# Delta rule in 64x64 tiles, and a mixer's front in another order

## The reference

```python
qkv = jax.nn.silu(_causal_dwconv(proj[..., OFF_Q:OFF_Z], conv_w))
g = -jnp.exp(dn_a_log) * jax.nn.softplus(a + dn_dt_bias); beta = jax.nn.sigmoid(b)
# per chunk of CHUNK = 64 tokens and per head (4 heads of 128)
g_cum = jnp.cumsum(g, axis=-1)
decay = jnp.exp(jnp.where(causal, g_cum[..., :, None] - g_cum[..., None, :], -jnp.inf))
lower = jnp.where(strict, jnp.einsum("bnhcd,bnhsd->bnhcs", kb, k) * decay, 0.0)
tmat = jnp.eye(CHUNK) + lower
sol = lax.linalg.triangular_solve(tmat, rhs, left_side=True, lower=True)   # u and w
attn = jnp.where(causal, jnp.einsum("bnhcd,bnhsd->bnhcs", q, k) * decay, 0.0)
# then a scan over the four chunks with u, w, attn, qg, k_dec and the state s
# S5: x_t = A x_{t-1} + B u_t (complex, diagonal), y = Re(C x_t) + D u_t
```

## Time and profile before

| what | value |
|---|---|
| median of three runs | 1792.93 us (1792.62 to 1793.97) |
| the profiled execution: time | 1791.53 us |
| the profiled execution: span | 1789.8 us |
| mean granted TensorE clock | 0.997 |
| TensorE busy | 1763.8 us, 99% of the span |
| VectorE, ScalarE, GpSimd busy | 1042.8, 827.8, 77.8 us |

### The profile page before, as it was taken

One profiled execution on the slowest core, in us unless ns is written; L12 is line 12 of the kernel. 1 busy time (PEld: TensorE's weight loads), 2 busy tenths in 40 slices (PEclk: granted clock), 3 DMA queues, 4 the chain that ended last, 5 costly groups with the idle time before them and its releaser, 6 DMA issues.

```text
span 1789.8 us, 26939 instructions
## 1 busy us (share of the span) xinstructions
PE 1763.8 (99%) x11356; PEld 1568.9 (88%) x11356; DVE 1042.8 (58%) x1218; ACT 827.8 (46%) x914; POOL 77.8 (4%) x145
## 2 busy tenths in 40 slices
PE   8999999999999999999999999999998999999998
PEld 8998797888999899987978879998888976889996
DVE  5445466977644455554669776455676535645553
ACT  5544355553654355543555636545123124545542
POOL 0000000000000000000000001000471100000000
PEclk9999999999999999999999999999999999999999
DMA  7547255444654645472545448855244314346371
GB/s 259 188 148 267 82 181 164 156 141 149 228 188 188 211 142 188 129 281 87 180 156 163 143 142 212 198 193 209 95 166 80 114 52 132 128 155 207 108 283 58
DMA packets 194331, 293.13 MB, mean 164 GB/s; under 512 B 9298, under 2 KB 128884, under 8 KB 194244
## 3 DMA queue, kind: packets, MB, share of 16 engines
q1 hardware_dynamic: 191988, 287.72, 47.7%
q0 software_dynamic: 1936, 4.14, 2.1%
q10 hardware_dynamic: 320, 0.01, 0.0%
HBM read 289.49 MB, written 2.36 MB: 163 GB/s over the span
## 4 chain that ended last, share of the span: by engine, by line
PE 92%; DVE 4%; DMA 2%; issue 1%; ACT 1%; ACTq 0%; DVEq 0%; SPq 0%
PE acc L233 24%; PE acc L234 23%; PE acc L235 23%; PE acc L280 3%; PE acc L216 2%; DMA ring<-in_ffn_w_in 1%; PE acc L3086 1%; PE acc L488 1%; PE acc L2777 1%; PE acc L201 1%; PE acc L262 1%; PE turn L368 1%; PE acc L1338 1%; PE turn L1443 1%; PE turn L2850 1%
## 5 line engine op out<-in xcount | busy, mean ns | idle before, releaser
L455 DVE TENSOR_TENSOR w_lo<-ring,w_hi 128x2048 fp32r<-128x2048 f32 x160 | 361.7, 2290 | 207.7 <-ACT w_hi L451 207.7
L233 PE MATMUL acc<-xT_hi,w_hi 128*128 128x256 f32 x1680 | 476.9, 284 | 1.5 <-DVE xT_lo L386 0.8
L235 PE MATMUL acc<-xT_hi,w_lo 128*128 128x256 f32 x1680 | 476.3, 283 | 0.0
L234 PE MATMUL acc<-xT_lo,w_hi 128*128 128x256 f32 x1680 | 476.2, 283 | 0.0
L451 ACT ACTIVATE w_hi<-ring 128x2048 fp32r<-128x2048 f32 x160 | 301.0, 1911 | 142.4 <-PE acc L235 99.6
L233 PEld LDWEIGHTS acc<-xT_hi,w_hi 128*128 128x128 f32 x1680 | 323.0, 192 | 2.6 <-DVE xT_lo L386 1.8
L234 PEld LDWEIGHTS acc<-xT_lo,w_hi 128*128 128x128 f32 x1680 | 323.1, 192 | 0.0
L235 PEld LDWEIGHTS acc<-xT_hi,w_lo 128*128 128x128 f32 x1680 | 323.0, 192 | 0.0
L233 PE MATMUL acc<-w_hi,hT_hi 128*128 128x512 f32 x440 | 172.7, 393 | 0.0
L235 PE MATMUL acc<-w_hi,hT_lo 128*128 128x512 f32 x440 | 171.6, 390 | 0.0
L234 PE MATMUL acc<-w_lo,hT_hi 128*128 128x512 f32 x440 | 171.5, 390 | 0.0
(11 more groups left out here) (553 smaller groups left out, 2944.2 us busy)
## 6 DMA issues: line engine op xcount, KB each, us to landing
ring<-in_ffn_w_in SPq DMA_DIRECT2D x88, 1024.0 KB, 5.7
ring<-in_w_in SPq DMA_DIRECT2D x52, 1024.0 KB, 5.0
ring<-in_ffn_w_out SPq DMA_DIRECT2D x44, 1024.0 KB, 6.4
ring<-in_w_branch SPq DMA_DIRECT2D x12, 1024.0 KB, 5.0
ring<-in_w_out SPq DMA_DIRECT2D x12, 1024.0 KB, 5.0
ring<-in_w_gate SPq DMA_DIRECT2D x11, 1024.0 KB, 5.1
ring<-in_w_up SPq DMA_DIRECT2D x11, 1024.0 KB, 6.5
ring<-in_w_down SPq DMA_DIRECT2D x11, 1024.0 KB, 6.8
```

What stands on the lines that cost most here:

```text
L233: pe.matmul(o, a_hi, wh, start=start, stop=False)
L234: pe.matmul(o, a_hi, wl, start=False, stop=False)
L235: return pe.matmul(o, a_lo, wh, start=False, stop=stop)
L455: vec.tensor_tensor(w_part(w_lo, r), raw_part(c0, r), w_part(w_hi, r).bitcast(F32), ALU.subtract).then_inc(f.lo, 1)
```

## The change

It does four things.

The delta rule's block matrices lose their zero blocks: they become 128 partitions by 64 columns, chunk b of a row tile in partitions 64b to 64b+63. Masks shrink likewise (`half_ident`, `half_upper`, copied on GpSimd at the program's start, `lvl`). Every product of two such matrices becomes two products of 64x64x64, one in each diagonal quarter of the array (`halves_pe`), both writing one PSUM bank. `dn_kk_pe` uses all 128 rows and two halves of 64 columns. The inverse's transposes become products with `half_ident`. VectorE's and ScalarE's operations there go from 512 to 256 columns.

In `rc_solve_pe` the second half now takes 64 rows at a time, chunk b to bank `turn[2 + b]`, and both banks are complete only with its last products.

The taps come ahead on all three engines: on VectorE ahead of the convolutions of keys and queries, on TensorE ahead of the values' products, on ScalarE ahead of the convolutions' activations. The memory's transposes move behind the first quarter of the values' products; the convolution of queries moves behind the memory's evictions.

The decay and the first four copies come between the two halves of the scan on VectorE; on TensorE the decay's sums come ahead of the fills, and one fill fewer stands ahead of `s5_y_pe`.

```diff
+        half_ident = sb("half_ident", [P, CH])
+        half_upper = sb("half_upper", [P, CH])
...
+        HALVES = 9
...
-        attnT = big(23588, 8, P)
+        attnT = big(23588, 8, CH)
...
-        X = big(20480, 8, P)
+        X = big(20480, 8, CH)
...
         def s5_taps_pe(pe):
             pe.wait_ge(sk.vec, TAPS)
+            pe.wait_ge(sw.act, 8)
...
+
+        def s5_scanned_vec(vec):
             vec.wait_ge(s5.vec, 5)
...
-                    ins = pe.matmul(turn[m][:, h * P:(h + 1) * P], g2[:, j:j + 1].broadcast_to([P, P]), ublk[:, :],
-                                    start=True, stop=True)
+                    for b in range(2):
+                        rows = half_rows(b)
+                        ins = pe.matmul(turn[m][rows, h * CH:(h + 1) * CH], g2[rows, j:j + 1].broadcast_to([CH, CH]),
+                                        half_upper[rows, :], start=True, stop=True)
...
-        def dn_turn_vec(vec):
-            for r in range(6):
+        def dn_copies_vec(vec, r0, r1):
+            for r in range(r0, r1):
...
+            for bank0, other in ((0, kbT), (2, qnT)):
+                for m in range(MT):
+                    for h in range(DH):
+                        for b in range(2):
+                            toks = slice(m * P + CH * b, m * P + CH * b + CH)
+                            ins = pe.matmul(turn[bank0 + m][half_rows(b), h * CH:(h + 1) * CH], knT[:, h, toks], other[:, h, toks],
+                                            start=True, stop=True)
+                    ins.then_inc(dn.pe, 1)
...
+        def halves_pe(pe, o, m, left, right):
+
+            for h in range(DH):
+                for b in range(2):
+                    rows = half_rows(b)
+                    ins = pe.matmul(o[rows, h * CH:(h + 1) * CH], left[rows, 4 * m + h, :], right(rows, 4 * m + h), start=True, stop=True)
+            return ins
...
+            for j in range(8):
+                for b in range(2):
+                    rows = half_rows(b)
+                    ins = pe.matmul(turn[2 + b][:, j * CH:(j + 1) * CH], kbe[rows, j // 4, (j % 4) * P:(j % 4 + 1) * P], XT[rows, j, :],
                                     start=True, stop=True)
-                ins.then_inc(rc.pe, 1)
+                    if j == 7:
+                        ins.then_inc(rc.pe, 1)
...
-            pe.wait_ge(rc.act, 1 + m)
+            pe.wait_ge(rc.act, 1 + n % 2)
...
-            pe.wait_ge(sw.act, 8)
-            norm_pe(pe, nmem, nb=memx)
-            turned_group_pe(pe, G_V2, C_V2, xT, 4, 512)
+            s5_taps_pe(pe)
+
+            def memory_turned(pe, half):
+                if half == 0:
+                    pe.wait_ge(sk.act, 1)
+                    norm_pe(pe, nmem, nb=memx)
+            turned_group_pe(pe, G_V2, C_V2, xT, 4, 512, between=memory_turned)
             z2_right_pe(pe)
             s5_state_pe(pe)
-            s5_taps_pe(pe)
             z2_left_pe(pe, 0)
             z2_left_pe(pe, 1)
+            dn_cs_pe(pe)
             fill(2)
-            dn_cs_pe(pe)
-            fill(1)
             dn_turn_pe(pe)
             fill(1)
...
+            s5_u_act(act)
+            s5_taps_act(act)
             conv2_act2(act, 0)
+            conv2_act1(act, 2)
             conv2_act2(act, 1)
-            s5_u_act(act)
-            conv2_act1(act, 2)
             z2_right_act(act)
-            s5_taps_act(act)
...
-            def conv_kq(vec):
+            def taps_and_conv_k(vec):
+                s5_taps_vec(vec)
                 conv2_vec(vec, 0)
-                conv2_vec(vec, 1)
...
-            s5_taps_vec(vec)
+            conv2_vec(vec, 1)
             conv2_vec(vec, 2)
             ab_vec(vec)
             s5_scan_vec(vec)
             dn_cs_vec(vec)
+            dn_copies_vec(vec, 0, 4)
+            s5_scanned_vec(vec)
+            dn_copies_vec(vec, 4, 6)
             dn_turn_vec(vec)
```

More of the change, by code:

```diff
@@ L806, in const_pool @@
                                pattern=[[-1, P]], channel_multiplier=1).then_inc(cst.pool, 1)
+            pool.wait_ge(cst.pool, 5)
+            for b in range(2):
+                rows = half_rows(b)
+                pool.tensor_copy(half_ident[rows, :], ident[rows, rows]).then_inc(cst.pool, 1)
+                pool.tensor_copy(half_upper[rows, :], upper[rows, rows]).then_inc(cst.pool, 1)
+            pool.wait_ge(cst.pool, 9)
+        HALVES = 9
         def const_vec(vec):
@@ L1868, in build @@
         HD = 128
-        CH = 64
         NS = 16
@@ L2826, in inv_start_act @@
                 act.wait_ge(iv.pe, 1 + m)
[L2827 removed]
+                act.activation(quad(X, m), heads(turn[m][:, 0:TOK], 4), ACT.Copy).then_inc(iv.act, 1)
         def inv_level_act(act, i):
@@ L2831, in inv_level_act @@
                 act.wait_ge(iv.pe, inv_p(i) + 1 + m)
-                act.activation(quad(Y, m), heads(turn[m][:, :], 4), ACT.Copy).then_inc(iv.act, 1)
+                act.activation(quad(Y, m), heads(turn[m][:, 0:TOK], 4), ACT.Copy).then_inc(iv.act, 1)
+        def halves_pe(pe, o, m, left, right):
+            for h in range(DH):
+                for b in range(2):
+                    rows = half_rows(b)
+                    ins = pe.matmul(o[rows, h * CH:(h + 1) * CH], left[rows, 4 * m + h, :], right(rows, 4 * m + h), start=True, stop=True)
+            return ins
         def inv_start_pe(pe):
@@ L2836, in inv_start_pe @@
                 pe.wait_ge(iv.vec, 2 + 2 * m)
-                for h in range(DH):
-                    ins = pe.transpose(turn[m][:, h * P:(h + 1) * P], XT[:, 4 * m + h, :], ident[:, :])
-                ins.then_inc(iv.pe, 1)
+                halves_pe(pe, turn[m], m, XT, lambda rows, j: half_ident[rows, :]).then_inc(iv.pe, 1)
         def inv_level_pe(pe, i, between):
@@ L2847, in inv_level_pe @@
                     pe.wait_ge(iv.vec, inv_v(i - 1) + 3 + 2 * m)
-                for h in range(DH):
-                    j = 4 * m + h
-                    ins = pe.matmul(turn[m][:, h * P:(h + 1) * P], CT[i % 2][:, j, :], X[:, j, :], start=True, stop=True)
-                ins.then_inc(iv.pe, 1)
+                halves_pe(pe, turn[m], m, CT[i % 2], lambda rows, j: X[rows, j, :]).then_inc(iv.pe, 1)
             between(0)
@@ L2859, in inv_level_pe @@
                 if i < 5:
-                    for h in range(DH):
-                        j = 4 * m + h
-                        ins = pe.matmul(turn[m][:, h * P:(h + 1) * P], XT[:, j, :], Y[:, j, :], start=True, stop=True)
-                    ins.then_inc(iv.pe, 1)
-                for h in range(DH):
-                    j = 4 * m + h
-                    ins = pe.matmul(turn[2 + m][:, h * P:(h + 1) * P], Y[:, j, :], XT[:, j, :], start=True, stop=True)
-                ins.then_inc(iv.pe, 1)
+                    halves_pe(pe, turn[m], m, XT, lambda rows, j: Y[rows, j, :]).then_inc(iv.pe, 1)
+                halves_pe(pe, turn[2 + m], m, Y, lambda rows, j: XT[rows, j, :]).then_inc(iv.pe, 1)
             between(1)
@@ L2874, in rc_solve_pe @@
                 for h in range(DH):
-                    ins = pe.matmul(turn[m][:, h * P:(h + 1) * P], XT[:, 4 * m + h, :], v_tok2[:, m, h * P:(h + 1) * P],
-                                    start=True, stop=True)
-                ins.then_inc(rc.pe, 1)
-            for m in range(MT):
-                for h in range(DH):
-                    ins = pe.matmul(turn[2 + m][:, h * P:(h + 1) * P], kbe[:, m, h * P:(h + 1) * P], XT[:, 4 * m + h, :],
-                                    start=True, stop=True)
-                ins.then_inc(rc.pe, 1)
+                    for b in range(2):
+                        rows = half_rows(b)
+                        ins = pe.matmul(turn[m][rows, h * P:(h + 1) * P], XT[rows, 4 * m + h, :], v_tok2[rows, m, h * P:(h + 1) * P],
+                                        start=True, stop=True)
+                ins.then_inc(rc.pe, 1)
+            for j in range(8):
+                for b in range(2):
+                    rows = half_rows(b)
+                    ins = pe.matmul(turn[2 + b][:, j * CH:(j + 1) * CH], kbe[rows, j // 4, (j % 4) * P:(j % 4 + 1) * P], XT[rows, j, :],
+                                    start=True, stop=True)
+                    if j == 7:
+                        ins.then_inc(rc.pe, 1)
         def rc_rows(n):
@@ L2914, in rc_o_pe @@
                     pe.matmul(o, qgT[:, h, n * CH:(n + 1) * CH], S2[n][:, h * P:(h + 1) * P], start=True, stop=False)
-                ins = pe.matmul(o, attnT[rows, 4 * m + h, rows], u_sol[rows, 4 * m + h, :], start=(n == 0), stop=True)
+                ins = pe.matmul(o, attnT[rows, 4 * m + h, :], u_sol[rows, 4 * m + h, :], start=(n == 0), stop=True)
             if n % 2 == 1:
@@ L2984, in rc_act @@
         def rc_act(act):
-            for m in range(MT):
-                act.wait_ge(rc.pe, 3 + m)
-                act.activation(quad(wT, m), heads(turn[2 + m][:, :], 4), ACT.Copy).then_inc(rc.act, 1)
+            for b in range(2):
+                act.wait_ge(rc.pe, 3 + b)
```

(1 more changed line is left out.)

58 lines of the change are left out of this document (28 added, 30 removed).

## The result

The median of seven runs is 1800.11 us (1795.36 to 1802.85) against 1792.89 before: a ratio of 1.0037, 95% interval 1.0027 to 1.0048. The change costs 7.2 us. I had forecast 1791.8, a gain of 1.1, with a range of 1784 to 1798.

The account below looks back on a forecast made before the run. The prediction took TensorE, busy 99% of the span, as the bound: -9.5 us behind the scan and +8.4 in the reordered front make -1.1, so the median goes from 1792.93 to 1791.8 us, range 1784 to 1798.

Parts of the forecast that it names:

- The tiles: Everything behind the scan: 64x64 products in pairs, changed solution and moved fill together save 9.5 us.
- the moved fill: One 1.75 us fill moves from before the scan to behind `rc_out_pe` and covers L233's wait: -0.95 us.
- The levels: The inverse's five levels on TensorE: 7.0 us a level instead of 8.8, -8.2 us in all.
- the solution and the first state: `rc_solve_pe` unchanged in time, but the first state product waits for a 512-column ScalarE copy: +0.7 us.
- the last wait: TensorE's 0.95 us wait at L233, the first output product, forecast to be covered by a fill.
- the diagonal pairs do not overlap: Rival, 11%: a pair of 64x64x64 products costs 0.22 us, the inverse saves nothing; 1808 us.
- TensorE at the states: TensorE reaches `s5_state_pe` at 1342.5, after taps (2.0) and 22.8 us of other work.
- The rotations' end: GpSimd's rotations, slowed by the taps' products on VectorE, end at 1335.5 to 1338.5 instead of 1322.2.
- u's landing: u is back from DRAM at 1347.7 to 1352.5, taken as 1349: TensorE waits 6.5 us at the states.
- `s5_y_pe` at S + 28.8, with a wait of some 6: S is u's landing; VectorE's copies between the scan's halves make TensorE wait some 6 us before `s5_y_pe`.
- The clock loss, 2.0 behind each wait: Lower granted clock costs TensorE 2.0 us after the wait at the states and again after `s5_y_pe`'s.
- u lands far later: Rival, 14%: last rotations fall under convolutions, u's DMAs share engines with weight loads; S = 1354, +5, 1797 us.

Follow-up runs that it names:

- the tiles alone: The changed kernel with all orders of the kernel before put back, keeping the 64x64 tiles: 1784.27 us, ratio 0.9951.
- the kernel before with its wait filled: The kernel before with 12 products that nobody reads in its 5.17 us wait ahead of the q, k, v transposes: 1792.21 us, ratio 0.9997.
- the order alone: The kernel before, on 128x128 blocks, with the change's new order and split of the scan put in: 1808.3 us, ratio 1.0078.
- after with the rows broken up: After with each half's fill in `s5_y_pe` moved into the middle of its 16 narrow products, waits unfilled: 1798.13 us, ratio 1.0029.
- its ten with the waits filled: After with 22 and 13 products that nobody reads in its waits for u and for the scan: 1794.66 us, ratio 1.0011.
- the split alone: After with taps, memory transposes and convolutions back where they were; decay and four copies stay between the scan's halves: 1792.13 us, ratio 0.9992.
- with u moved early: After with GpSimd storing u behind the sixth and loading it behind the seventh of eight rounds of rotations: 1788.47 us, ratio 0.9972.

## Where the prediction was right and where it failed

**The tiles** (-9.5, of which 0.95 by the moved fill): right. In the tiles alone, from `dn_turn2_pe` to the first output product it is 96.80 us, against 105.52: -8.7, forecast -8.55. The levels take 33.7 for 42.3, so -8.6 (forecast -8.2); from `dn_turn2_pe` to the first level 1.1 less (1.1); the solution and the first state 1.0 more (0.7); and in after the last wait is gone. A pair of products costs 0.126 with its share of the shape changes, not 0.22, so the rival "the diagonal pairs do not overlap" is out. The Trainium skill's rule in "TensorEngine Tiling (Array Packing)", "Restrictions and Gotchas", that different row tiles cannot access one PSUM bank at once, would by the prediction's rival have brought 1808; no run here shows such a price, with both halves in one bank.

**TensorE at the states** by 1342.5: right, 1343.8 less the 1.1 of the start. **The rotations' end** between 1335.5 and 1338.5: right, 1336.45 (1335.4 without the late start). The row with 2.5 us a step agrees with the Trainium skill's exclusive lock ("SBUF — State Buffer", "SBUF: two separate sides").

**u's landing** at 1349, at most 1352.5: the first step that failed. From the rotations' end to the landing I took 12.2 us from before, and at most 2 more for the weight loads. It took 16.9, because the store landed after 7.7 us instead of 3.5. It had moved to a stretch in which the DMA engines were 0.95 busy and two weight loads of 1 MB were issued; in before its stretch (1322.5 to 1326.0) was 0.74 busy. The states began at 1353.5, or 1352.4 without the late start: 3.4 late, at the far end of the bounds that I had stated.

**`s5_y_pe` at S + 28.8, with a wait of some 6:** right. 1353.5 + 28.8 = 1382.3, it was 1381.92, and the wait is 6.18. The chain of copies between the halves of the scan was read rightly.

**The clock loss, 2.0 behind each wait:** the step that failed most. I took the loss that follows before's wait as a fixed price, and had none anywhere else. In the profiled execution it was 1.5 at the states, 9.4 in `s5_y_pe` and 1.7 at the solution. From `s5_y_pe`'s start to `dn_turn2_pe` I had counted 21.4 us; it took 28.64.

Added to the forecast span of 1788.7: 1.1 for the start, 3.4 for u, -0.4 for the way to `s5_y_pe`, 7.2 in it, 0.9 behind it and 0.3 from the first output on make 1801.2; it was 1801.1. In the median the miss is 8.3 us. No median execution was traced; if u was as late there, 3.4 are from u, and the mean granted clock (0.991, against 0.989 in the profiled one) puts most of the rest on the clock too. The nearest rival was "u lands far later", 1797. Half of its cause came true: the DMAs met the weight loads, but the rotations ended when forecast. No case had the clock cost more than 2 us at a time, and the range ended at 1798 for that.

**What stays open** is what makes the clock fall in work without a wait, as at 1400.9 in after and at 1375.3 in the kernel before with its wait filled. The small tiles aren't needed for it: that kernel has none, and neither has the order alone, where a fall came at 1400.5. The narrow rows remain a candidate. Ten traces have twelve falls in the mixer's front with no wait over 0.4 us in the 10 us ahead; eleven began in a row of 16 products (32 instructions) with 32 columns or within 0.6 us behind it, the twelfth (1393.3 in after with the rows broken up) at the end of a row with 64 columns. But most such rows ran at full clock, so the rows don't decide it alone, and no run takes them away. Filled waits keep off only a part. Where TensorE waits 6 to 10 us the falls are more and longer: in the mixer only kernels with such a wait have stretches of 10.2 or 13.7 us, and after's seven executions have a mean granted clock of 0.989 to 0.992, its ten with the waits filled 0.993 to 0.999. What decides in which execution a fall comes isn't shown.

## What to carry to other kernels

When a step moves on one engine, walk down the queue of every engine that it can slow, to the last DMA at its end: here products on VectorE held up GpSimd's arithmetic (2.5 us a step), and with it a transfer that stood behind it and that TensorE waited for. A step put between two halves of a chain is paid by whoever waits for the second half; look whether that consumer has work that needs only the first inputs, and move its wait behind that work. And price a wait of several microseconds on TensorE with the work behind it at half speed for as long as the traces show (3 to 12 us of work behind waits of 5 to 10 us here), not with one row's loss.

## What the runs showed of the hardware

- Two 64x64x64 products in diagonal quarters of the array overlap, writing other partitions of one PSUM bank: 0.126 us a pair, shape changes included, where a full 128x128x128 product takes 0.223. In the solution's second half, 32 instructions of 64 rows by 128 columns, the two row halves in turn into two banks, take 2.0 us (1462.41 to 1464.41), where 16 of the full array took 1.88.
- The granted clock fell to 0.50 in stretches of 3.4 to 13.7 us; over ten traces, twelve of them began with no wait of TensorE over 0.4 us in the 10 us ahead.
- The store of u landed after 3.5 us at 1322 and after 7.7 at 1337, with the DMA engines 0.74 and 0.95 busy. The taps' last load landed at 1370.3 to 1371.8, whether it was issued at 1354.8 (before), 1355.9 (the split alone) or 1360.5 (after); with u moved early it was issued at 1352.4 and landed at 1365.0.
